# Differential attention: unnormalised maps, pre-scaled queries, and one weight split inside instead of three

## The reference, cut to what matters

```python
s = jnp.einsum('bqhmd,bkhmd->bhmqk', qblk, k) * scale        # scale = 64 ** -0.5, m = 0, 1
p = jax.nn.softmax(s, axis=-1)
a = p[:, :, 0] - lam * p[:, :, 1]
o = jnp.einsum('bhqk,bkhe->bqhe', a, vf)
...
o = rmsnorm(o, subln_g, SUBLN_EPS) * (1.0 - lambda_init)     # per head, over its 128 columns
x = x + g1 * (o.reshape(b, l, N_HEADS * V_DIM) @ w_o)
```

## Time and profile before

| | |
|---|---|
| time, median of 3 runs (range) | 1531.51 us (1530.84 to 1533.18) |
| profiled execution: time; span from first to last instruction | 1532.66 us; 1530.8 us |
| busy: TensorE, VectorE, ScalarE, GpSimd | 1435.9, 1062.6, 818.5, 186.0 us |
| chain that ended last, share of TensorE, VectorE, ScalarE | 86%, 8%, 2% |
| mean granted TensorE clock | 0.972 |
| mean DMA rate | 264 GB/s |

### The profile page before, as it was taken

How to read it: one execution, slowest core, us unless ns; L and a number is a source line. 1 busy time by engine, 2 the same in 40 slices (tenths; PEclk the granted TensorE clock), 3 DMA queues, 4 the chain that set the end, 5 groups by cost and what they waited for, 6 DMA issues and landing times.

```text
span 1530.8 us, 17395 instructions
## 1 busy us (share of the span) xinstructions
PE 1435.9 (94%) x6951; PEld 1167.7 (76%) x6951; DVE 1062.6 (69%) x1037; ACT 818.5 (53%) x814; POOL 186.0 (12%) x296
## 2 busy tenths in 40 slices
PE   5899876999999998998899999999999999999994
PEld 1777444788999995677688888888888888888873
DVE  0642675545555556434789998899988999889994
ACT  2422554433222324224667777677777777777761
POOL 4000243000000001000895000000000000000000
PEclk9999998999999999996999999999999999999996
DMA  9846554373434346233789999999999999999971
GB/s 347 308 164 235 213 200 172 136 249 110 138 111 137 110 143 228 72 121 137 264 306 397 374 370 376 357 410 356 374 372 355 409 362 367 376 358 394 371 286 43
DMA packets 115479, 406.07 MB, mean 265 GB/s; under 512 B 7649, under 2 KB 30354, under 8 KB 97986
## 3 DMA queue, kind: packets, MB, share of 16 engines
q1 hardware_dynamic: 109040, 384.34, 67.0%
q0 software_dynamic: 5280, 17.34, 3.7%
q10 hardware_dynamic: 1074, 3.23, 0.5%
HBM read 394.92 MB, written 9.96 MB: 264 GB/s over the span
## 4 chain that ended last, share of the span: by engine, by line
PE 86%; DVE 8%; ACT 2%; DMA 2%; issue 2%; POOL 0%; DVEq 0%; SPq 0%; ACTq 0%
PE ps L1479 25%; PE ps L1481 25%; PE ps L1480 25%; PE ps L1493 2%; DMA raw<-in_ada_w 2%; DVE ring_lo L1294 2%; PE ps L1719 1%; PE ps L1802 1%; PE ps L1541 1%; PE ps L1520 1%; PE ps L1665 1%; PE ps L1783 1%; DVE mx L1142 1%; ACT prob L781 0%; PE ps L1732 0%
## 5 line engine op out<-in xcount | busy, mean ns | idle before, releaser
L1294 DVE TENSOR_TENSOR ring_lo<-raw,ring_hi 128x2048 fp32r<-128x2048 f32 (+1 forms) x210 | 451.9, 2167 | 66.1 <-ACT ring_hi L870 65.4
L870 ACT ACTIVATE ring_hi<-raw 128x2048 fp32r<-128x2048 f32 (+1 forms) x210 | 381.8, 1820 | 142.8 <-PE ps L1481 142.1
L1479 PE MATMUL ps<-ring_hi,xe 128*128 128x512 f32 (+1 forms) x576 | 219.1, 380 | 6.6 <-DVE eh L1373 4.0
L1007 DVE TENSOR_TENSOR ring_lo<-raw,ring_hi 128x2048 fp32r<-128x2048 f32 x53 | 120.4, 2289 | 144.9 <-ACT ring_hi L685 144.9
L1481 PE MATMUL ps<-ring_lo,xe 128*128 128x512 f32 (+1 forms) x576 | 217.0, 377 | 0.0
L1480 PE MATMUL ps<-ring_hi,xe 128*128 128x512 f32 (+1 forms) x576 | 216.7, 376 | 0.0
L685 ACT ACTIVATE ring_hi<-raw 128x2048 fp32r<-128x2048 f32 x53 | 101.3, 1912 | 182.3 <-PE ps L1481 149.0
L1294 DVE TENSOR_TENSOR ring_lo_more<-raw,ring_hi_more 128x2048 fp32r<-128x2048 f32 (+1 forms) x70 | 151.7, 2168 | 18.2 <-ACT ring_hi_more L870 17.9
L870 ACT ACTIVATE ring_hi_more<-raw 128x2048 fp32r<-128x2048 f32 (+1 forms) x70 | 127.4, 1820 | 42.4 <-PE ps L1481 42.2
L1479 PEld LDWEIGHTS ps<-ring_hi,xe 128*128 128x128 f32 x576 | 108.8, 189 | 24.6 <-DVE eh L1373 4.4
L1481 PEld LDWEIGHTS ps<-ring_lo,xe 128*128 128x128 f32 x576 | 108.4, 188 | 17.8
(11 more groups left out here) (272 smaller groups left out, 2367.5 us busy)
## 6 DMA issues: line engine op xcount, KB each, us to landing
raw<-in_w_gu_e SPq DMA_DIRECT2D x128, 1024.0 KB, 7.5
raw<-in_w_down_e SPq DMA_DIRECT2D x88, 1024.0 KB, 8.2
raw<-in_ada_w SPq DMA_DIRECT2D x48, 1024.0 KB, 5.7
raw<-in_w_gu_e SPq DMA_DIRECT2D x64, 768.0 KB, 6.6
raw<-in_w_gu SPq DMA_DIRECT2D x44, 512.0 KB, 4.9
raw<-in_w_qkv SPq DMA_DIRECT2D x12, 1024.0 KB, 12.7
raw<-in_w_down SPq DMA_DIRECT2D x11, 1024.0 KB, 6.6
raw<-in_w_o SPq DMA_DIRECT2D x4, 1024.0 KB, 5.2
```

The source lines that it names most:

```text
L870: act.activation(ehi[m % RINGM][:, 0:w], raw[:, (MOE_U0 + m) % RAW, 0:w], ACT.Copy).then_inc(hi_ready, 1)
L1007: dve.tensor_tensor(ring_lo[:, s % RING, :], raw[:, u % RAW, :], ring_hi[:, s % RING, :].bitcast(F32), ALU.subtract).then_inc(lo_ready, 1)
L1294: dve.tensor_tensor(elo[m % RINGM][:, 0:w], raw[:, (MOE_U0 + m) % RAW, 0:w], ehi[m % RINGM][:, 0:w].bitcast(F32), ALU.subtract).then_inc(l ...
L1479: pe.matmul(out, l_hi, r_hi, start=first, stop=False)
```

## The change

Five edits go together.

1. The maps are subtracted without normalising: with row sums s0 and s1 the kernel forms `p0 - (lam * s0 / s1) * p1` of the bare exponentials, s0 times the reference's map. The head norm takes the factor out again, if its epsilon is multiplied by the square of s0; GpSimd does this with one more operation for each item (`o_eps`). `lam` is kept negated, and the row sums of every item are kept.
2. Queries are multiplied by the scale as they are copied, so the row maximum is negated by the reduction itself, and `exps` has no scale.
3. The keys' copy moves from ScalarE to VectorE, behind the queries'.
4. The group 1 modulation units begin one projection unit earlier. VectorE's part of the group comes within the projection loop, and its transposes stand inside the last projection unit. For items with i % 3 equal to 0, `out_rows(i - 3)` stands first in VectorE's iteration.
5. One unit of the output projection is split inside the attention, not three: ScalarE's half is behind item 19, VectorE's half behind item 21. The second is split on ScalarE ahead of the gate copies, the third and fourth behind them. The stream's order follows.

```diff
-ADA_FROM = len(QKV_UNITS) - KC
+ADA_FROM = len(QKV_UNITS) - KC - 1
-SPLIT_WO_AT = (17, 19, 21)
+SPLIT_WO_AT = (19,)
...
@@ GpSimd, each item
+                pool.wait_ge(exp_done, i + 1)
+                pool.tensor_scalar(o_eps[:, k, h:h + 1], sums[:, i, 0:1], sums[:, i, 0:1], SUBLN_EPS,
+                                   ALU.mult, ALU.mult).then_inc(o_ep, 1)
+                pool.wait_ge(o_ep, i + 1)
                 pool.wait_ge(o_sum, i + 1)
-                pool.tensor_scalar(o_msq[:, k, h:h + 1], o_ssq[:, k, h:h + 1], 1.0 / P, SUBLN_EPS,
+                pool.tensor_scalar(o_msq[:, k, h:h + 1], o_ssq[:, k, h:h + 1], 1.0 / P, o_eps[:, k, h:h + 1],
                                    ALU.mult, ALU.add).then_inc(o_ms, 1)
@@ ScalarE
-            def keys_turned(h):
-                act.wait_ge(qkT_ps, h + 1)
-                if h >= 2:
-                    act.wait_ge(score_ps, 3 * (h - 1))
-                act.activation(kT[:, h % 2, :], ps[:, 6, :], ACT.Copy).then_inc(kT_sb, 1)
...
-                                         bias=nmx[:, i % 2, m:m + 1], scale=SCALE,
-                                         accum_out=sums[:, i % 2, m:m + 1])
+                                         bias=nmx[:, i % 2, m:m + 1], accum_out=sums[:, i, m:m + 1])
...
+            split_hi(WO0 + 1)
             for j in range(4):
                 keep_gate(0, j)
-            for s in range(WO0 + 3, FFN0 + 2):
+            for s in range(WO0 + 2, FFN0 + 2):
                 split_hi(s)
@@ VectorE
+                if s == 10:
+                    ada_rows_out(1)
+                    ada_cols_out(1)
...
-                dve.tensor_copy(qT[:, h % 2, :], ps[:, 5, 0:TOK]).then_inc(qT_sb, 1)
+                dve.tensor_scalar(qT[:, h % 2, :], ps[:, 5, 0:TOK], SCALE, None, ALU.mult).then_inc(qT_sb, 1)
+                dve.tensor_copy(kT[:, h % 2, :], ps[:, 6, :]).then_inc(kT_sb, 1)
...
-                link(dve.tensor_reduce(mx[:, i % 2, :], ps[:, 2 * (i % 2):2 * (i % 2) + 2, 0:n], AX.X, ALU.max))
-                dve.tensor_scalar(nmx[:, i % 2, :], mx[:, i % 2, :], -SCALE, None, ALU.mult).then_inc(negmax, 1)
+                dve.tensor_reduce(nmx[:, i % 2, :], ps[:, 2 * (i % 2):2 * (i % 2) + 2, 0:n], AX.X, ALU.max,
+                                  negate=True).then_inc(negmax, 1)
...
-                link(dve.reciprocal(rs[:, i % 2, :], sums[:, i % 2, :]))
-                link(dve.tensor_scalar(l1[:, i % 2:i % 2 + 1], rs[:, i % 2, 1:2], lam[:, 0:1], None, ALU.mult))
-                link(dve.tensor_scalar(prob[:, i % 2, 1, 0:n], prob[:, i % 2, 1, 0:n], l1[:, i % 2:i % 2 + 1], None, ALU.mult))
+                link(dve.reciprocal(rs[:, i % 2:i % 2 + 1], sums[:, i, 1:2]))
+                link(dve.tensor_scalar(l1[:, i % 2:i % 2 + 1], rs[:, i % 2:i % 2 + 1], sums[:, i, 0:1], lam[:, 0:1],
+                                       ALU.mult, ALU.mult))
...
-                dve.scalar_tensor_tensor(amap[:, i % 2, 0:n], prob[:, i % 2, 0, 0:n], rs[:, i % 2, 0:1],
-                                         prob[:, i % 2, 1, 0:n], ALU.mult, ALU.subtract).then_inc(a_ready, 1)
+                dve.scalar_tensor_tensor(amap[:, i % 2, 0:n], prob[:, i % 2, 1, 0:n], l1[:, i % 2:i % 2 + 1],
+                                         prob[:, i % 2, 0, 0:n], ALU.mult, ALU.add).then_inc(a_ready, 1)
...
             for i in range(ITEMS + 3):
+                if i >= 3 and i % 3 == 0:
+                    out_rows(i - 3)
                 if i + 1 < ITEMS:
                     row_max(i + 1)
                 if i < ITEMS:
                     difference(i)
-                if i >= 3:
+                if i >= 3 and i % 3:
                     out_rows(i - 3)
...
-                if i in SPLIT_WO_AT:
-                    split_lo(WO0 + SPLIT_WO_AT.index(i))
+                if i - 2 in SPLIT_WO_AT:
+                    split_lo(WO0 + SPLIT_WO_AT.index(i - 2))
...
-            split_lo(WO0 + 3)
+            for s in range(WO0 + 1, WO0 + 4):
+                split_lo(s)
@@ TensorE
-                project(QKV0, n, kh, s, (n % 2) * 3, qkv_acc, 2 * n, hlo_ready if s == 0 else None, 0)
-                if s >= ADA_FROM:
+                project(QKV0, n, kh, s, (n % 2) * 3, qkv_acc, 2 * n, hlo_ready if s == 0 else None, 0,
+                        (lambda k: ada_turn(1) if k == 1 else None) if s == len(QKV_UNITS) - 1 else None)
+                if ADA_FROM <= s < ADA_FROM + KC:
                     ada_unit(1, s - ADA_FROM)
...
-            ada_turn(1)
             turn_heads(0)
```

More of the change, by code:

```diff
@@ L86, in stream_before_experts @@
         s.append(u)
-        if i >= ADA_FROM:
+        if ADA_FROM <= i < ADA_FROM + KC:
             s.append(("ada", 1, i - ADA_FROM))
@@ L196, in build @@
         o_rstd = sb("o_rstd", [P, TILES, HEADS])
-        mx = sb("mx", [P, 2, 2])
         nmx = sb("nmx", [P, 2, 2])
-        sums = sb("sums", [P, 2, 2])
-        rs = sb("rs", [P, 2, 2])
+        sums = sb("sums", [P, ITEMS, 2])
+        rs = sb("rs", [P, 2])
+        o_eps = sb("o_eps", [P, TILES, HEADS])
         l1 = sb("l1", [P, 2])
@@ L355, in build @@
             sem, ("qkT_ps", "qT_sb", "kT_sb", "score_ps", "negmax", "exp_done", "a_ready", "aT_ps", "aT_sb", "o_ps", "o_sb"))
-        o_sum, o_ms, o_rs, on_ready = map(sem, ("o_sum", "o_ms", "o_rs", "on_ready"))
+        o_ep, o_sum, o_ms, o_rs, on_ready = map(sem, ("o_ep", "o_sum", "o_ms", "o_rs", "on_ready"))
         gbc_ps, gbc_sb, proj_acc = map(sem, ("gbc_ps", "gbc_sb", "proj_acc"))
@@ L791, in map_turned @@
                 act.activation(aT[:, i % 2, 0:n], ps[:, 4, 0:n], ACT.Copy).then_inc(aT_sb, 1)
-            keys_turned(0)
             exps(0)
@@ L799, in _ @@
                     exps(i + 1)
-                if i % 3 == 0 and i // 3 + 1 < HEADS:
-                    keys_turned(i // 3 + 1)
                 if i >= 3:
@@ L1029, in _ @@
             dve.wait_ge(lam_exp, 1)
-            link(dve.tensor_scalar(lam[:], lams[:, 2:3], lams[:, 3:4], LAMBDA_INIT, ALU.subtract, ALU.add))
+            link(dve.tensor_scalar(lam[:], lams[:, 3:4], lams[:, 2:3], LAMBDA_INIT, ALU.subtract, ALU.subtract))
             def ada_rows_out(g):
@@ L1159, in out_rows @@
                 dve.tensor_copy(obuf[:, k, h * P:(h + 1) * P], ps[:, 5, TOK:HALF]).then_inc(o_sb, 1)
-            ada_rows_out(1)
-            ada_cols_out(1)
             queries_turned(0)
```

## The result

| | before | after |
|---|---|---|
| time, median (range), 4 runs each | 1531.69 us (1530.84 to 1533.18) | 1496.28 us (1495.95 to 1499.79) |
| ratio, 95% interval | | 0.9775 [0.9761, 0.9789] |

The change saves 35.4 us by the medians, 2.25% by the ratio. After's profiled execution took 1499.79 us, 3.5 above its median, so the traces show about 3 us less of the gain than the medians.

The account below looks back on a forecast made before the run. TensorE, busy 94% of the span, was taken to bound the kernel. Terms of -0.2 (entry), -6.05 (plain heads), -13.8 (last heads), +0.8 (GpSimd) and +0.3 (gates) summed to -19.0 us: 1513 us, range 1508 to 1519.

Parts of the forecast that it names:

- all stages after the projection as long as now: Sign: the stages behind the output projection keep their length, a forecast difference of 0.
- Five plain heads: Attention items 3 to 17: each head takes 8.20 us instead of 9.41, in all -6.05 us.
- Two last heads: End of attention: one split inside instead of three, 21.05 us instead of 34.86, so -13.8.
- edits 1 and 2: Prediction's numbering, each head: scaling pass gone (0.45 us) and output copy ahead of the row maximum (0.76 us).
- Entry: Start of attention: moving modulation ahead gains nothing; later scores +0.45, less negation 0.19 and pass 0.45: -0.2 us.
- GpSimd's operation: After the last map: one more small op of 0.27 us in each of three items, +0.8 us.
- Gates: After attention: ScalarE splits one unit before keeping the first gate, so TensorE waits, +0.3 us.
- B: Rival, heads: the hoisted copy comes late and transposes start no sooner; 0.76 x 7 heads return, 1518 us, chance 0.13.
- C: Rival: the one split costs as much as each of three and the moved ones hold TensorE; 1516.5 us, chance 0.11.
- D: Rival: clock stays up through entry and last head (3 us), a half split is hidden (1.5); 1507 us, chance 0.05.
- E: Rival: TensorE's clock stays low through attention, costing 2.8 us a head; slower, up to 1543 us, chance 0.03.
- F: Rival: nothing arrives because later stages absorb the gain; 1531 us, chance 0.02.

Follow-up runs that it names:

- u_split3: The changed kernel with three output projection splits inside attention again, at the old items, VectorE's half at once: 1510.71 us.
- a_pad32: The changed kernel with 32 unused bytes ahead of h_hi, large tiles 32 past a multiple of 64 as before the change (place 96): 1509.59 us.
- u_entry: The changed kernel with group 1's modulation units, sums and transposes back where they were: 1497.16 us.
- b_pad224: The kernel before with 224 unused bytes ahead of lmax, putting later tiles at the changed kernel's addresses (place 64): 1520.68 us.
- b_pad32: The kernel before with 32 unused bytes ahead of h_hi, large tiles at a multiple of 128 bytes (place 128): 1510.31 us.
- u_keys: The changed kernel with the keys' copy back on ScalarE: 1496.26 us.

## Why the prediction was wrong, point by point

**The failed step** is the last clause of what would show it, "all stages after the projection as long as now", and the list of parts behind it. The list went through the instructions that the edits add and remove and passed over the tiles they declare. Those moved the stationary operands of the dense matmuls from a distance of 32 bytes to one of 64, which shortened each step from 233.4 to 229.5 ns: 11.0 to 13.3 us over the kernel, against 0 forecast. The trace of before had the sign of it: its fourth slot ran at 230 ns in the mean, 226 to 228 behind the run-in, beside 233 for the others.

**The size of the edits** was forecast as 19.0 and measures 22.1, 24.4 and 18.6 at the places 96, 64 and 128. At before's own place they give 1509.6, within the range. That the sum fits is in part luck, since single terms missed both ways. By the columns of the table for equal places:
- *Five plain heads*: -6.37 against -6.05. Right in sum and in the rows of the new head. A plain head gained 1.14 (9.42 to 8.28), not 1.21; the first of the five gained 1.38 and the one with the gate group 1.55 (10.67 to 9.12), which the forecast did not have. The split of the 1.21 was less right: undoing the pass costs 0.39 (0.45 forecast), undoing the hoisted copy 0.3 (0.76 forecast). Some 0.5 of the 1.14 appears in neither; no run undoes both, so whether the two hide each other is not shown.
- *Two last heads*: 18.1 to 18.6 us instead of 21.05, the mis-sized term. "VectorE's 2.29 stands between the query copy and the row maximum of item 23, whole on the chain" was wrong: at item 21 there is no next head, so neither transposes nor query copy come there, and the half split runs beside TensorE's modulation pair. The head with both halves and the gate group, items 20 to 23, took 10.31, 2.03 above a plain one, where 4.64 was forecast (1.45, 2.29 and 0.9); the one with ScalarE's half at its end (215.92) took 8.28 as the others.
- *Three splits against one*: the 13.8 forecast for the two heads held the gain of edits 1 and 2 in them, 2.4 at 1.21 a head. The splits' own share was thus 11.4, and u_split3 shows 11.8 in these heads. Its expectation of 13.8 for the time counted the 2.4 in, so that its 14.4 lies near is no proof of the term.
- *Entry*: -0.28 between before and a_pad32, -0.2 forecast; u_entry agrees. But seven traces of after and its variants at place 64 (u_entry among them) have 122.0 to 125.0 in that stretch and b_pad224 has 123.6, so a difference this small is within the scatter, and after's 121.98 against before's 126.13 is the operands' place, the clock and scatter, not shown to be the edit. The parts show more. From the head transposes to the first scores it is 2.32 instead of 1.71 (+0.6, forecast +0.45). From there to the map of item 2, at full clock, it is 7.87 (after, u_entry) instead of 8.47 (b_pad32, b_pad224), so 0.60 less (forecast 0.64); before itself, with a low stretch in it, has 10.04.
- *GpSimd's operation*: +1.3 at full clock (9.25 to 10.58), not +0.8, and +2.15 to +2.8 in the traces of a_pad32 and after. Items became 1.97 long, not 1.8, because the operation takes 0.27 and the next one, which now reads its addend from a tile, grew from 0.19 to 0.26. What lies beyond the 1.3 goes with the low clock (0.56 in after while the last rows are turned) and, in after, items that began 0.6 later.
- *Gates*: +0.9 at place 96 and +0.3 at the two others, against +0.3. The prediction's own terms give +0.2 (264.7 less 264.49).
- *Keys*: nothing, as forecast; u_keys shows it.

**The rivals.** B, the wait only exchanged: no, the wait for the copy is gone, though undoing the hoist alone costs only 0.3 a head. C, the one split as dear as each of three: no. D, "More than that comes", had the right sign. Of its two mechanisms the hidden half split is in the trace, with some 2.5 us; a gain by the clock at the entry isn't shown, at an equal place. Its terms, 3 and 1.5, lead from 1513 to 1508.5 and not to its 1507. Neither mechanism is what brought most of the 16.7 us beyond the forecast. E, a low clock in attention: in after the clock was 1.00 from 157 to 205. The Trainium skill ("TensorE: Matmul & The Clock Gate", HAM oscillation) warns of waits between bursts; after's trace shows low stretches only at the last gate group and at the end of attention. One trace shows E on a small scale in a plain head: b_pad224 has 0.50 from 199.8 to 203.2, and that head took 11.05 instead of 9.43. F: the gain arrived whole.

## What to carry to other kernels

A change that adds or resizes a small tile moves every tile declared behind it, and that can be worth more than the edit. Compare a change with a version of the old kernel whose large tiles lie at the same addresses, or first pin both operands of the dense matmuls to the same remainder by 256 bytes. Where instructions, operands' names and clock are equal and the step between matmuls still differs by a few ns, look at the addresses.

## What was not expected of the hardware

- The step between dense 512-column fp32r matmuls, each with its own weight load, depends on the distance by 256 bytes between the moving tile and the stationary one: 227.2 ns at 0, 229.5 at -64, 233.3 to 233.5 at +64, +32 and -32. Other distances were not run. Between 0 and -32 it is 14.3 us of the expert stage alone (765.3 and 779.6).
- The Trainium skill ("TensorE: Matmul & The Clock Gate", Step-by-step: what each phase is for) says that loading the next weights takes no SBUF read bandwidth from the running matmul, and gives 216 ns as the back-to-back gap of 512 columns, without naming fp32r. The runs differ: no ring slot's stream of 512-column fp32r matmuls with their own weight loads averaged less than 227, and with nothing changed but the distance between the two tiles read, the step grew to 233. That the two reads disturb each other would fit; no run shows it directly. The measurement decides.
- A small GpSimd operation took 0.19 us with constants and 0.26 to 0.27 with a factor or addend read from a tile; on VectorE the lambda operation went from 0.21 to 0.27 with a second multiplication by such an operand.
